# Feed-forwards 0 to 3: one 512-column product for the high weights, and an addition of the bank's halves on DVE

## What is computed

```
def swiglu(x, w_gate, w_up, w_down):
    return (jax.nn.silu(x @ w_gate) * (x @ w_up)) @ w_down

    for l in range(DEPTH):
        h = h + 0.5 * swiglu(rms_norm(h, ffn1_norm[l]), ffn1_w_gate[l], ffn1_w_up[l], ffn1_w_down[l])
        h = h + hybrid_mixer(rms_norm(h, mix_norm[l]), w_in[l], ...)
        h = h + 0.5 * swiglu(rms_norm(h, ffn2_norm[l]), ffn2_w_gate[l], ffn2_w_up[l], ffn2_w_down[l])
```

## Time and profile before

| | us |
|---|---|
| median of 3 runs (3034.6 to 3036.47) | 3036.05 |
| span of the profiled execution | 3033.5 |
| PE busy in it | 2858.9 |
| DVE busy | 1641.2 |
| ACT busy | 1220.4 |

### The profile page before, as it was taken

How to read it: one execution, slowest core, us unless ns; L and a number is a source line. 1 busy time by engine, 2 the same in 40 slices (tenths; PEclk the granted TensorE clock), 3 DMA queues, 4 the chain that set the end, 5 groups by cost and what they waited for, 6 DMA issues and landing times.

```text
span 3033.5 us, 64798 instructions
## 1 busy us (share of the span) xinstructions
PE 2858.9 (94%) x27888; PEld 2392.3 (79%) x27888; DVE 1641.2 (54%) x2465; ACT 1220.4 (40%) x1864; POOL 112.1 (4%) x152
## 2 busy tenths in 40 slices
PE   8999999999999999998868999998998999998998
PEld 8987799899877997776656777785456998985986
DVE  5546655454565555213564777646234564565885
ACT  5445554444455545322443432334103434432333
POOL 0000000000000000000000000000001222220000
PEclk9999999999999999997988999999999999999999
DMA  6544345554543454441001333321210000003443
GB/s 251 181 176 163 137 153 182 180 181 176 185 153 124 175 182 150 181 153 70 2 10 56 120 144 141 123 87 62 84 56 16 5 5 24 5 4 112 140 153 111
DMA packets 50412, 349.82 MB, mean 115 GB/s; under 512 B 5840, under 2 KB 5840, under 8 KB 9808
## 3 DMA queue, kind: packets, MB, share of 16 engines
q1 hardware_dynamic: 49680, 343.56, 31.8%
q0 software_dynamic: 448, 2.11, 0.2%
HBM read 344.61 MB, written 1.05 MB: 114 GB/s over the span
## 4 chain that ended last, share of the span: by engine, by line
PE 81%; DVE 13%; ACT 3%; issue 2%; DMA 1%; DVEq 0%; ACTq 0%; SPq 0%
PE psum L165 80%; DVE arena L98 3%; DVE ring_low L87 2%; DVE arena L87 2%; DVE wide L87 2%; DMA ring<-in_evt 1%; PE psum L170 1%; DVE wide L98 1%; DVE ring L87 1%; ACT w_high L144 1%; ACT wide L138 0%; ACT arena L140 0%; ACT x_high L138 0%; ACT arena L144 0%; DVE arena L94 0%
## 5 line engine op out<-in xcount | busy, mean ns | idle before, releaser
L87 DVE TENSOR_TENSOR ring_low<-ring,w_high 128x2048 fp32r<-128x2048 f32 (+3 forms) x254 | 560.3, 2206 | 554.1 <-ACT w_high L144 549.3
L144 ACT ACTIVATE w_high<-ring 128x2048 fp32r<-128x2048 f32 (+3 forms) x254 | 468.9, 1846 | 766.0 <-PE psum L165 452.9
L165 PE MATMUL psum<-x_high,w_high 128*128 128x256 f32 (+1 forms) x2040 | 632.8, 310 | 8.1 <-DVE arena L87 6.3
L165 PE MATMUL psum<-x_high,ring_low 128*128 128x256 f32 (+1 forms) x2040 | 625.9, 307 | 0.0
L165 PE MATMUL psum<-x_low,w_high 128*128 128x256 f32 (+1 forms) x2040 | 625.7, 307 | 0.0
L165 PEld LDWEIGHTS psum<-x_high,w_high 128*128 128x128 f32 x2040 | 389.5, 191 | 45.6 <-issue 17.1
L165 PEld LDWEIGHTS psum<-x_high,ring_low 128*128 128x128 f32 x2040 | 389.6, 191 | 18.4
L165 PEld LDWEIGHTS psum<-x_low,w_high 128*128 128x128 f32 x2040 | 389.7, 191 | 16.8
L165 PE MATMUL psum<-wide,ring 64*64 64x64 f32 (+3 forms) x3888 | 384.4, 271 | 12.2 <-DVE wide L87 7.6
L165 PEld LDWEIGHTS psum<-wide,ring 64*64 64x64 f32 (+2 forms) x3888 | 269.6, 147 | 108.6 <-issue 78.0
L165 PE MATMUL psum<-w_high,x_high 128*128 128x512 f32 (+2 forms) x720 | 282.2, 392 | 10.4 <-issue 8.0
(11 more groups left out here) (196 smaller groups left out, 3421.1 us busy)
## 6 DMA issues: line engine op xcount, KB each, us to landing
ring<-in_f_gu SPq DMA_DIRECT2D x88, 1024.0 KB, 4.8
ring<-in_w_mod SPq DMA_DIRECT2D x48, 1024.0 KB, 5.0
ring<-in_fu SPq DMA_DIRECT2D x44, 1024.0 KB, 4.8
ring<-in_f_dn SPq DMA_DIRECT2D x40, 1024.0 KB, 4.8
ring<-in_w_in SPq DMA_DIRECT2D x28, 1024.0 KB, 4.8
ring<-in_fd SPq DMA_DIRECT2D x20, 1024.0 KB, 4.9
ring<-in_rkvr SPq DMA_DIRECT2D x12, 1024.0 KB, 4.8
ring<-in_w_out SPq DMA_DIRECT2D x8, 1024.0 KB, 4.9
```

The source lines that it names most:

```text
L87: self.done(self.eng.tensor_tensor(o, a, b, op), then)
L144: self.done(self.eng.activation(o, i, ACT.Copy, scale=scale), then)
L165: ins = self.eng.matmul(o, l, r, start=a, stop=z)
```

## The change

In feed-forwards 0 to 3, `x_high` and `x_low` become the two planes of one tensor `x_both` (at the addresses they had). For each k-step, the high weights meet both planes in one matmul of 512 columns, which fills the whole bank: `w_high` by `x_high` in columns 0 to 255, `w_high` by `x_low` in columns 256 to 511. The low weights meet `x_high` in a second matmul of 256 columns into the first half. The two halves of the bank must then be added: `halves_added` is a `tensor_reduce` on DVE whose innermost dimension has two elements, 256 apart, and which writes 128x256 to SBUF (`gsum` for the gate, `usum` for the up half, four and two buffers in a free part of the arena). SiLU now reads `gsum` after `gsum_ok`, and the product reads `sil` and `usum`. The banks are free again with `gsum_ok` and `usum_ok`. Feed-forwards 4 and 5 stay as they were.

```diff
@@ -314,8 +314,8 @@
         ring = at("ring", [128, NSLOT, WS], RING)
         ring_low = at("ring_low", [128, NSLOT, WS], RING, F32R)
         w_high = at("w_high", [128, HIGHS, WS], WHIGH, F32R)
-        x_high = at("x_high", [128, 4096], XHIGH, F32R)
-        x_low = at("x_low", [128, 4096], XLOW, F32R)
+        x_both = at("x_both", [128, 2, 4096], XHIGH, F32R)
+        x_high, x_low = x_both[:, 0, :], x_both[:, 1, :]
         h_high = at("h_high", [128, 22, 256], ARENA, F32R)
         h_low = at("h_low", [128, 22, 256], ARENA + 5632, F32R)
         arena = at("arena", [128, AN], ARENA)
@@ -612,6 +612,7 @@
         conv_ok = signal("conv_ok", [(i, f) for i in (4, 5) for f in range(22)])
         gelu_ok = signal("gelu_ok", [(i, f) for i in (4, 5) for f in range(22)])
         prod_ok = signal("prod_ok", [(i, f) for i in FFNS for f in range(22)])
+        gsum_ok, usum_ok = [signal(n, [(i, f) for i in range(4) for f in range(22)]) for n in ("gsum_ok", "usum_ok")]
         hh_ok = signal("hh_ok", [(i, u) for i in FFNS for u in range(12 if i == 4 else 22)])
         hl_ok = signal("hl_ok", [(i, u) for i in FFNS for u in range(12 if i == 4 else 22)])
         ya_ok = signal("ya_ok", [(i, n, tb) for i in (4, 5) for n in range(2) for tb in ((0, 2) if i == 4 else (0,))])
@@ -619,6 +620,8 @@
 
         sil = arena[:, 11264:12288].rearrange("p (a t) -> p a t", a=4)
         prod = arena[:, 12288:13312].rearrange("p (a t) -> p a t", a=4)
+        gsum = arena[:, 16384:17408].rearrange("p (a t) -> p a t", a=4)
+        usum = arena[:, 17408:17920].rearrange("p (a t) -> p a t", a=2)
         hT = arena[:, 0:11264].rearrange("p (k t) -> p k t", k=22)
         IMG = arena[:, 11264:12056].rearrange("p (i r c) -> p i r c", i=2, r=6)
         IMC = arena[:, 12056:12572].rearrange("p (i c) -> p i c", i=2)
@@ -665,7 +668,7 @@
                 wt = (high(key), low(key)) if is_split(key) else ()
                 for half in range(2):
                     b = 2 * (f % 3) + half
-                    T.bank(b, prod_ok[i, f] if half else (silu_ok[i, f] if i < 4 else img_ok[i, f]))
+                    T.bank(b, (usum_ok if half else gsum_ok)[i, f] if i < 4 else prod_ok[i, f] if half else img_ok[i, f])
                     for k in range(8):
                         if f == 0 and half == 0:
                             for q in norms:
@@ -675,9 +678,12 @@
                             T.mm(bank(b)[:, 0:tok], raw(key)[:, o:o + 128], x_whole[:, k, :], k == 0, k == 7,
                                  None if k < 7 else w_free(key) if half else gate_mm((i, f)))
                             continue
-                        mms(T, products(bank(b)[:, 0:tok], [y[:, o:o + 128] for y in wt],
-                                        [x_hi[:, k, :], x_lo[:, k, :]], k == 0, k == 7),
-                            None if k < 7 else w_free(key) if half else gate_mm((i, f)))
+                        then = None if k < 7 else w_free(key) if half else gate_mm((i, f))
+                        if i >= 4:
+                            mms(T, products(bank(b)[:, 0:tok], [y[:, o:o + 128] for y in wt],
+                                            [x_hi[:, k, :], x_lo[:, k, :]], k == 0, k == 7), then)
+                            continue
+                        wide_product(T, b, wt, o, k, k == 0, k == 7, then)
                 if i == 4:
                     n, part = mod_parts(f)
                     if part < 2:
@@ -725,6 +731,18 @@
                     elif i == 4 and n == 0 and g == 2:
                         mod_turn_pe(T, 1, 11)
 
+        def wide_product(T, b, wt, o, k, first, last, then):
+
+            both = x_both[:, :, 256 * k:256 * k + 256]
+            if first:
+                T.mm(bank(b), wt[0][:, o:o + 128], both, True, False)
+            T.mm(bank(b)[:, 0:256], wt[1][:, o:o + 128], both[:, 0, :], False, False)
+            if not first:
+                T.mm(bank(b), wt[0][:, o:o + 128], both, False, last, then)
+
+        def halves_added(D, o, b, then):
+            D.red(o, bank(b).rearrange("p (j t) -> p t j", j=2), ALU.add, then)
+
         def ffn_act(A, i):
             se = A.eng
             lat0 = 256 if i == 4 else 0
@@ -740,12 +758,13 @@
                 norm_act(A, q)
             for f in range(22):
                 bg = bank(2 * (f % 3))
-                se.wait_ge(*gate_mm[i, f])
                 if i < 4:
+                    se.wait_ge(*gsum_ok[i, f])
                     if f >= 4:
                         se.wait_ge(*prod_ok[i, f - 4])
-                    A.act(sil[:, f % 4, :], bg[:, 0:256], ACT.Silu, silu_ok((i, f)))
+                    A.act(sil[:, f % 4, :], gsum[:, f % 4, :], ACT.Silu, silu_ok((i, f)))
                 else:
+                    se.wait_ge(*gate_mm[i, f])
                     if f >= 2:
                         se.wait_ge(*conv_ok[i, f - 2])
                     else:
@@ -877,11 +896,16 @@
                 if i == 4 and f and mod_parts(f - 1)[1] == 2:
                     mod_dve(D, 1, mod_parts(f - 1)[0])
                 if i < 4:
+                    ve.wait_ge(*gate_mm[i, f])
+                    if f >= 4:
+                        ve.wait_ge(*silu_ok[i, f - 4])
+                    halves_added(D, gsum[:, f % 4, :], 2 * (f % 3), gsum_ok((i, f)))
+                    ve.wait_ge(*w_free["gu", i, f])
+                    halves_added(D, usum[:, f % 2, :], 2 * (f % 3) + 1, usum_ok((i, f)))
                     ve.wait_ge(*silu_ok[i, f])
-                    ve.wait_ge(*w_free["gu", i, f])
                     if f >= 4:
                         ve.wait_ge(*hh_ok[i, f - 4])
-                    D.tt(product_of(i, f), sil[:, f % 4, :], bank(2 * (f % 3) + 1)[:, 0:256], ALU.mult, prod_ok((i, f)))
+                    D.tt(product_of(i, f), sil[:, f % 4, :], usum[:, f % 2, :], ALU.mult, prod_ok((i, f)))
                     if f:
                         low_part(D, i, f - 1)
                 else:
```

## The result

The changed kernel takes 3050.34 us (median of 4 runs, 3048.99 to 3053.9), the kernel before 3035.32 beside it (4 runs). The ratio is 1.0048, with a 95% interval of 1.0036 to 1.0061, so the change costs 15.0 us. The forecast was 3048.4. The profiled executions differ by 16.2 us of span, 3049.7 against 3033.5.

What follows compares the result with a forecast made beforehand. PE's matmuls were taken to bound the kernel before, a closed ACT-DVE path after. Feed-forward shifts of 4.11, 2.18, 3.48 and 2.55 us, together +12.3, on 3036.05 gave 3048.4 us; range 3033 to 3062 us.

Steps and rivals of the forecast that it cites:

- What bounds the kernel: Before the change, a feed-forward is as long as PE's list of matmuls; PE holds 81% of the span.
- PE's saving: Gate/up tiles: one 512- and one 256-column product replace three of 256; 5.547 instead of 5.76 us, 18.8 us in all.
- the ring: Closed path per gate/up tile: ACT split, DVE split, gate reduction, SiLU, `high_part`, next ACT split; 6.12 us against PE's 5.547.
- The reduction: 176 added DVE reads of 128x512 of PSUM, forecast at 0.69 us each, 122 us of DVE in all.
- that rival (+59 us): Strided PSUM read takes a second cycle per element: reduction 1.23 us, +59.2 us, 3095.3 us; chance 0.13 including prices near it.
- The waits of PE: PE waits about 0.57 us at tile heads for DVE's `ring_low`, from tiles 10 to 13 to the third down tile.
- The clock: Rival: PE's clock falls in the gaps, PE idling about 0.4 us per tile; no size given, chance 0.03.
- By feed-forward: Shift of PE at the third down tile in feed-forwards 0 to 3: 4.11, 2.18, 3.48 and 2.55, together +12.3 us.
- the D of the forecast: End of DVE's last split ahead of a feed-forward's first product, before the change: 25.82, 413.61, 609.50 and 996.85 us.
- That the gain arrives: Rival: the ring takes under 5.55 us, so PE bounds again; -18.8 us, 3017.3 us; chance 0.08 in part or whole.

## Why the prediction held, step by step

**What bounds the kernel** held: PE before, the path between ACT and DVE after. The decisive reading was to ask, of each moved wait, what stands ahead of the releasing instruction on its own engine, and not how full DVE is.

**PE's saving** was sized 0.213 us a tile, 18.8 in all; it is 5.76 - 5.59 = 0.17, or 15.0 us, and the kernels with the ring cut have 13.0 to 16.2 in the four feed-forwards (one of them 9.8, see above). That spread is the clock, as is shown below; the three in which as many feed-forwards begin at 1.2 GHz as in the kernel before have 14.5 to 14.8. The term mis-sized is the wide product, taken from a down tile. It had no part in the sum, as the prediction says: the ring sets the end whatever PE's tile is. By the Trainium skill (VectorE: DVE Perf Modes, "The TRN2 errata") the saving was an estimated 3.5 us; the runs don't agree, with about 15.

**The reduction** was sized 0.69 and is 692 ns, to the nanosecond that of the row with 512 elements side by side. The reading with elements 256 apart costs nothing, and that rival (+59 us) fell. The rule of the Trainium skill on lines (SBUF — State Buffer, "Specifications (TRN2)"), by which every element would lie on a new line of PSUM, shows no effect on DVE here (692 ns either way).

**The ring** was 6.12 and is 6.11 for the first tiles, 6.14 from then on. Part by part, forecast and measured: 1.94 and 1.95, 2.43 and 2.42, 0.72 and 0.73, 0.51 and 0.51, 0.52 and 0.53. The step to 6.14 comes with the tiles where the reduction has one wait more, for the SiLU four tiles back (`f >= 4`), and it lies where that wait is: from DVE's split to the reduction it is 2.40 up to tile 3 (but for one late turn, below) and 2.42 to 2.43 from tile 4 on, in all four feed-forwards. With 18 such turns of 21 it is 0.37 us a feed-forward over the forecast, 1.5 in all. (The hand-over from DVE to ACT was written as 0.03, where its rows give 0.20 - 0.18 = 0.02; measured in the ring it is 0.04, from 142.29 + 0.69 to 143.02.)

**The waits of PE** were forecast as about 53, 31 us in all, from tiles 10 to 13 on; they are 51 with 31.7 us, in feed-forward 0 from tile 10 on. **The clock** did not fall in these gaps (1.00 from 30 to 200 us, in the row above).

**By feed-forward** the time moved as follows (us, norm to norm):

| feed-forward | before | after | moved | forecast |
|---|---|---|---|---|
| 0 | 195.63 | 200.55 | +4.92 | +4.11 |
| 1 | 194.60 | 196.23 | +1.63 | +2.18 |
| 2 | 194.60 | 198.16 | +3.56 | +3.48 |
| 3 | 196.60 | 200.74 | +4.14 | +2.55 |
| sum | 781.43 | 795.68 | +14.25 | +12.3 |

The rest of the 16.2 us of span is in the two mixers (+1.8 and -0.5) and ahead of the first norm and behind the last feed-forward (+0.6 together), stages that the change doesn't touch. Two things moved single feed-forwards against the forecast. The first is late turns of the ring. In number 0 one turn takes 6.84, here on ACT:

```profile
38.96 1.92 ACT L144 ACTIVATE w_high<-ring 128x2048 fp32r<-128x2048 f32 x1
44.46 0.42 ACT L138 ACTIVATE arena<-arena 128x256 f32<-128x256 f32 x1 [3.58 <-DVE arena L106]
44.97 0.42 ACT L144 ACTIVATE h_high<-arena 128x256 fp32r<-128x256 f32 x1
45.80 1.92 ACT L144 ACTIVATE w_high<-ring 128x2048 fp32r<-128x2048 f32 x1 [0.41 <-ACT h_high L144]
```

The SiLU waits 0.4 longer for a reduction that is itself late, and the split starts 0.3 later behind `high_part` than in the other turns. In number 1 one turn takes 6.42, again with the split 0.3 late (463.25 to 469.67). They come at the same turns in the other kernels with the ring: 6.81 and 6.42 with three products; without the up reduction 6.41 and 6.42, with the split late and the reduction in time, and 6.52 and 6.49 at two further turns. What held them up the records don't show. In a ring such a slip isn't made up for, which is a price of its own of being on one. The 21 turns took 129.61, 129.17, 128.89 and 128.89 us where 128.52 was forecast: +1.09, +0.65, +0.37 and +0.37.

The second is the clock at the norms, where PE has gaps. The stretches of before and then of after (PEclk is the third number from the end):

```profile
402.50:406.50 4.00, 3.67 (x18) 3.70 (x19) 1.68 (x5) 1.42 (x3) 0.00 (x0) 0.57 0.47 199
985.00:993.00 8.00, 5.70 (x49) 5.73 (x50) 5.39 (x15) 5.30 (x14) 0.53 (x1) 1.00 0.55 205
```

```profile
405.00:415.00 10.00, 7.42 (x53) 6.58 (x52) 6.54 (x15) 7.12 (x18) 0.00 (x0) 1.00 0.35 125
998.00:1003.00 5.00, 4.39 (x25) 4.42 (x26) 2.25 (x6) 2.20 (x6) 0.00 (x0) 0.66 0.75 295
```

Before, the first work of feed-forward 1 ran for some 3.4 us at 1.2 GHz and that of feed-forward 3 at 2.4; after, it is the other way round. What that is worth can be read on DVE, from the start of the norm (L92) to the end of the last split ahead of the first product, the D of the forecast. In the changed kernel, feed-forwards 1 and 3:

```profile
408.98 0.61 DVE L92 TENSOR_SCALAR arena<-cst,nbuf 128x128 f32<-128x128 f32 x2 [0.27 <-ACT nbuf L138]
...
416.68 2.29 DVE L87 TENSOR_TENSOR ring_low<-ring,w_high 128x2048 fp32r<-128x2048 f32 x1 [1.41 <-ACT w_high L144]
...
998.18 0.61 DVE L92 TENSOR_SCALAR arena<-cst,nbuf 128x128 f32<-128x128 f32 x2 [0.27 <-ACT nbuf L138]
...
1007.08 2.29 DVE L87 TENSOR_TENSOR ring_low<-ring,w_high 128x2048 fp32r<-128x2048 f32 x1 [1.46 <-ACT w_high L144]
```

That is 9.99 and 11.19 us, where the kernel before has 11.22 and 9.98: the two have changed places. The forecast took its D from the kernel before, and with it that kernel's clock. In feed-forwards 0 and 2 the same stretch moved by -0.30 and -0.35 (14.12 to 13.82, 12.51 to 12.16). Forecast, clock and start, and turns of the ring add up to 4.11 - 0.30 + 1.09 = 4.90, 2.18 - 1.23 + 0.65 = 1.60, 3.48 - 0.35 + 0.37 = 3.50 and 2.55 + 1.21 + 0.37 = 4.13, against the measured 4.92, 1.63, 3.56 and 4.14. So nothing of the misses is left but 0.1 us. That the sum of the four came out within 2 us of the forecast is in part because the two shifts of the clock cancel.

The same two levels are in every kernel here: this stretch of feed-forwards 1 and 3 takes 9.98 to 9.99 us at a clock of 1.00, and 11.0 to 11.2 where 3.4 us of it are at 1.2 GHz. Most kernels have one of the two at 1.2 GHz. The one with ACT's split first has none, and its feed-forward 3 takes 192.89 us against 194.56 in the kernel with the gate reduction first; those with the narrow products in a row and without both reductions have both, and in the latter feed-forward 1 takes 190.91 against 189.34. These 1.6 us each way are the whole spread from 13.0 to 16.2.

**The rivals.** That the gain arrives is what happens as soon as the ring is cut; the forecast had put it at 5.55 us a turn, and the path would indeed have had to lose over half a microsecond. What decides it is where on DVE the added gate reduction stands, behind the split or ahead of it. A read that is slow, and a fall of the clock, fell.

## What to carry to other kernels

When work is put between two engines that each run a fixed list, write down the closed path from an instruction to its own next turn, through every wait and through what stands ahead on each engine, and add it up; if it is longer than the bound engine's turn, it is the new bound, however idle both engines are. Then put the new instruction ahead of the long one that doesn't need it (here 0.69 us ahead of 2.29, worth some 27 us), or move the long one on the other engine, and the same edit gains. Leaving out one added instruction at a time tells apart which is on the path and which only fills gaps. And before a difference of a microsecond or two in a single stage is explained, compare the granted clock at its start in both kernels.

## What the runs showed of the hardware beyond the forecast

- DVE reads PSUM with elements 256 apart as fast as side by side: 692 ns for 128x512, added up in pairs.
- A matmul of 512 columns of x takes 0.230 us where one of 512 columns of weights takes 0.227. Whether the 512 columns lie in one piece or in two makes no difference (5.59 us a tile either way).
- The turn of the ring is 0.02 to 0.03 us longer where the reduction on it has a wait more, even for a signal given long ago (6.11 and 6.14).
- The 3.4 us at 1.2 GHz behind a norm come at one feed-forward in one kernel and at another in the next, and cost 1.2 us up to the first product and 1.6 us of a feed-forward in which PE is the bound.
